# Differential attention: scores in three passes on split operands, value products one row later

## The chip, the cores and the metric

One core of a Trainium2 chip runs the whole program. The metric is the device time of one execution in microseconds (us). Three runs before the change took 2974.46, 2977.0 and 2977.47 us, median 2977.0.

## The reference

For a sequence of 1024 tokens of width 1024, three layers follow one another. The first has eight heads of forgetting attention (64 wide, causal, with a per-head decay added to the scores), a convolution and a pooling branch, then a feed-forward part. The second is retention. The third is differential attention. The two attentions matter here:

```python
# forgetting attention, for each block of 128 queries
s = einsum(q, k) * 64 ** -0.5 + cum[query] - cum[key]
p = softmax(where(key <= query, s, -1e30));  out = p @ v
# differential attention: 8 heads, each two halves of 64; q and k rotated (rope)
sc = einsum(q, k) * 64 ** -0.5          # for both halves
p = softmax(where(key_chunk <= query_chunk, sc, lowest))
out = (p[0] - lam * p[1]) @ v
```

Afterwards the output of a differential head is normalised over its 128 columns, scaled, and gated with a silu of a projection.

## The kernel before

Sizes: P = 128, S = 1024, NB = 8 blocks of 128 queries ("rows" t = 0 to 7), HALF = 512. The five engines run instruction streams of their own. The order on each is written out by hand, and they meet by counters: each finished step has a name (`s0_3`, `e1_2`, `pt0_4_1`), and the others wait for its number.

**Products to full precision.** The activations are split once into a high and a low part (HH, HL, type F32R), and each weight unit too (WH, WL; VectorE takes the difference at L255, `low_part`). `mm3` (L239 to L241) multiplies high by high, high by low and low by high into one sum. An F32 matmul on unsplit operands stands in the trace as two records, each with a weight load of its own.

**Attention.** `attend_pe`, `attend_act` and `attend_dve` serve both kinds. `forget` is true for the forgetting layer, where one iteration handles a pair of heads (three in a loop, the fourth in a last pass with `more` false). It is false for the differential layer, where one iteration is one head of two halves (seven in a loop, one last). For row t, TensorE does these steps:

- `projections(t)`: a part of the next head's q, k, v or gate, 24 matmuls of 512 columns for a whole half or 12 for part of one, into the bank DB. A plan by row says which.
- `turn(t)` (L764): the exponentials are transposed block by block into the banks TB, so that they can be stationary operands. With two forgetting heads this is done for head 0 and then head 1 through the same banks; the second waits until VectorE has copied the first into PT0 (L1056, `pt0_t_g`). A differential head has one set, the weights, which VectorE formed at L1035; it leaves the banks at L1051.
- `square_sums` (L794, forgetting only): sums of squares for the norm of the next q or k, into DB. ScalarE's copy and square precede them (L915, L917). Its logarithm (L923) and exponential (L925) follow, and DB is free for the next projection after the logarithm.
- `scores(t + 1)` (L810): both heads or halves, each on 64 of the 128 rows of the array, for the keys up to the row's end. Forgetting adds a bias (L818), and both add the mask (L822).
- `values(t)` (L852): the products of PT with the transposed v into the bank AO. They wait for `o{t-1}`, VectorE's output of the row before, which empties AO.

VectorE, for row t: copies out of the banks (`out_of_banks`), the gate (`gates`), the two row maxima of t + 1 (L1020), the scaled output (L1064 and L1066, or L1069), in the differential layer the weights of t + 1 (L1026 to L1035), the norm or rope of the next q or k, and in row 4 `low_part`. After row 7 come the copy of k into kT (L1099), `low_part`, and for a differential head its norm (L1981) and gating (L1987). ScalarE, for row t: the evacuation of a projection, then both exponentials of t + 1 (L960, in the order of the maxima), and at the head's end the silu, the copy of q into qT (L1010) and the squares of the output blocks (`block_out`, L1947).

Before the loops, `first_pe`, `first_act` and `first_dve` make the first head's q, k and v. q is copied at L1168 and k at L1190, and `warm` (L304) keeps TensorE busy. In the last forgetting pair `fill` puts the convolution's layer norm between the rows (`conv_pe`, L1222 and L1227; centring on VectorE at L1262, squares on ScalarE at L1236). In the last passes `warm` runs ahead of `turn`.

## Time and profile before

| | |
|---|---|
| median of 3 runs | 2977.0 us |
| profiled execution, in all | 2978.64 us |
| its span | 2976.6 us |
| TensorE busy | 2819.4 us (95%) |
| VectorE busy | 1609.3 us (54%) |
| ScalarE busy | 650.7 us (22%) |
| granted TensorE clock | 0.987 of full speed |

The span runs from the first to the last instruction of the profiled execution, and all later rows count from its start. Forgetting attention lies between about 172 and 496 us, differential attention between 2281 and 2856 us. A busy time is the union of an engine's instructions. What a change is worth depends on the engine that ends each wait, and so on the chain of waits.

### The profile page before, as it was taken

To read this page: it belongs to the slowest core of one execution; us is meant where nothing else is said; L and a number is where in the kernel's file an instruction comes from. 1 tells how busy PE (TensorE), PEld (TensorE's weight loads), DVE (VectorE), ACT (ScalarE), POOL (GpSimd) and SP (SyncE) were. 2 spreads that over 40 slices of the span, in tenths; PEclk is the share of its full clock that TensorE was granted. 3 is DMA by queue.
4 is the path that set the end of the run, shared out by engine and by line. 5 is a ranking of instruction groups with operands and counts; after the bars stand their busy time and mean duration, and the time that the engine had idled before them with its cause. 6 is when DMAs were issued, how large, how long until landed. Compare 5 with 4: busy or idle time off the path is not lost.

```text
span 2976.6 us, 35289 instructions
## 1 busy us (share of the span) xinstructions
PE 2819.4 (95%) x13352; PEld 2228.9 (75%) x13368; DVE 1609.3 (54%) x2062; ACT 650.7 (22%) x1152; POOL 299.1 (10%) x295
## 2 busy tenths in 40 slices
PE   8889999989999999999999999999998999999996
PEld 6656766768888888877888888888866777777664
DVE  7754445355554554564554454445374666666644
ACT  2133333121111111122111011011042333333321
POOL 0799700000000000001000000000000000000000
PEclk9999999999999999999999999999999999999998
DMA  4211111234443434333222222222242222222121
GB/s 165 88 38 57 56 43 71 99 113 143 140 155 127 165 139 146 141 113 142 85 70 85 85 70 70 92 77 79 77 170 89 71 70 70 71 72 71 50 113 71
DMA packets 48618, 286.61 MB, mean 96 GB/s; under 512 B 6576, under 2 KB 6704, under 8 KB 18608
## 3 DMA queue, kind: packets, MB, share of 16 engines
q1 hardware_dynamic: 21776, 118.50, 11.7%
q0 software_dynamic: 14544, 105.91, 10.4%
q10 hardware_dynamic: 12240, 61.39, 5.4%
q8 instruction: 40, 0.66, 0.1%
q14 instruction: 18, 0.15, 0.0%
HBM read 248.03 MB, written 29.36 MB: 93 GB/s over the span
## 4 chain that ended last, share of the span: by engine, by line
PE 81%; DVE 12%; issue 4%; ACT 2%; DMA 1%; DVEq 0%; SPq 0%; ACTq 0%
PE PB L239 12%; PE PB L241 12%; PE PB L240 12%; PE OBB L239 8%; PE OBB L241 8%; PE OBB L240 8%; PE OBB L852 3%; PE TBB L764 3%; PE PB L810 3%; PE TBB L239 2%; PE TBB L241 2%; PE TBB L240 2%; DVE small L1020 1%; DVE on L1830 1%; DVE cacc L1206 1%
## 5 line engine op out<-in xcount | busy, mean ns | idle before, releaser
L239 PE MATMUL PB<-HH,WH 128*128 128x512 f32 x1520 | 599.8, 395 | 25.6 <-issue 7.7
L241 PE MATMUL PB<-HH,WL 128*128 128x512 f32 x1520 | 594.8, 391 | 0.0
L240 PE MATMUL PB<-HL,WH 128*128 128x512 f32 x1520 | 594.8, 391 | 0.0
L239 PE MATMUL OBB<-HH,WH 128*128 128x512 f32 x992 | 399.6, 403 | 0.1
L241 PE MATMUL OBB<-HH,WL 128*128 128x512 f32 x992 | 387.3, 390 | 0.0
L240 PE MATMUL OBB<-HL,WH 128*128 128x512 f32 x992 | 386.7, 390 | 0.0
L239 PEld LDWEIGHTS PB<-HH,WH 128*128 128x128 f32 x1520 | 287.5, 189 | 93.1 <-issue 28.9
L240 PEld LDWEIGHTS PB<-HL,WH 128*128 128x128 f32 x1520 | 287.6, 189 | 61.9 <-issue 2.2
L241 PEld LDWEIGHTS PB<-HH,WL 128*128 128x128 f32 x1520 | 287.2, 189 | 60.5
L255 DVE TENSOR_TENSOR WL<-RAW,WH 128x2048 fp32r<-128x2048 f32 x101 | 233.1, 2308 | 61.9 <-DMA WH<-units 46.1
L2071 POOL DMA_DIRECT2D WH<-units x85 | 45.5, 535 | 1997.0 <-PE PB L239 1292.4
L241 PEld LDWEIGHTS OBB<-HH,WL 128*128 128x128 f32 x992 | 186.2, 188 | 40.2
L960 ACT ACTIVATE E<-PB,small 128x128 f32<-128x128 f32 (+3 forms) x192 | 140.8, 737 | 345.2 <-DVE small L1020 340.5
L239 PEld LDWEIGHTS OBB<-HH,WH 128*128 128x128 f32 x992 | 186.6, 188 | 35.9 <-DVE WL L255 0.3
L240 PEld LDWEIGHTS OBB<-HL,WH 128*128 128x128 f32 x992 | 186.7, 188 | 35.4
L1020 DVE TENSOR_REDUCE small<-PB 128x1 f32<-128x128 f32 (+3 forms) x192 | 136.2, 751 | 75.7 <-PE PB L822 75.7
L852 PE MATMUL OBB<-vt,PT 128*128 128x64 f32 (+1 forms) x1152 | 150.1, 281 | 11.2 <-DVE PT L1051 11.2
L852 PEld LDWEIGHTS OBB<-vt,PT 128*128 128x128 f32 x1152 | 137.7, 194 | 15.5 <-DVE PT L1051 15.5
L1551 DVE SCALAR_TENSOR_TENSOR G<-PB,par,G 128x1023 f32<-128x1023 f32 (+1 forms) x44 | 56.4, 1282 | 171.2 <-ACT G L1470 168.2
L2104 POOL TENSOR_TENSOR cacc<-cacc,prod 128x496 f32<-128x496 f32 (+29 forms) x90 | 131.2, 1459 | 0.0
L810 PE MATMUL PB<-kT,qT 64*128 64x512 f32 (+3 forms) x576 | 118.9, 517 | 4.9 <-DVE kT L1190 2.3
L764 PE MATMUL TBB<-con,E 128*128 128x128 f32 x576 | 88.5, 279 | 29.9 <-DVE PT L1056 19.6
(319 smaller groups left out, 3752.6 us busy)
## 6 DMA issues: line engine op xcount, KB each, us to landing
RAW<-units SPq DMA_DIRECT2D x85, 1024.0 KB, 4.8
WH<-units POOLq DMA_DIRECT2D x85, 1024.0 KB, 5.1
gs<-units ACTq DMA_DIRECT2D x16, 1024.0 KB, 4.8
gu<-gs ACTq DMA_DIRECT2D x16, 1024.0 KB, 3.9
RAW<-gu SPq DMA_DIRECT2D x16, 1024.0 KB, 4.8
WH<-gu POOLq DMA_DIRECT2D x16, 1024.0 KB, 5.4
tmpd<-xr SPq DMA_DIRECT2D x128, 64.0 KB, 2.0
A<-xT SPq DMA_DIRECT2D x4, 1024.0 KB, 9.8
```

The source lines that it names most:

```text
L239: first = pe.e.matmul(out, wh, xh, start=start, stop=False)
L240: pe.e.matmul(out, wh, xl, start=False, stop=False)
L241: return pe.e.matmul(out, wl, xh, start=False, stop=stop), first
L255: dve.e.tensor_tensor(WL[s][:, :], RAW[:, :], WH[s][:, :].bitcast(F32), ALU.subtract).then_inc(unit_split, 1)
L764: mm = pe.e.transpose(dst[:, c * P:(c + 1) * P], src(b), c_("ident"))
L810: pe.e.matmul(PB[c][:, b:b + w], qT[64 * c:64 * c + 64, t * P:(t + 1) * P], kT[64 * c:64 * c + 64, b:b + w], start=True, stop=False, skip_ ...
L852: mm = pe.e.matmul(AO[:, c * w:(c + 1) * w], (PT0, PT1)[c][:, b, :], vt[:, b, c * w:(c + 1) * w], start=b == 0, stop=b == t, skip_group_ch ...
L960: e.activation((E0, E1)[c][:, 0:n], PB[c][:, 0:n], ACT.Exp, bias=small[:, c, t:t + 1], accum_out=small[:, 2 + c, t:t + 1]).then_inc(act_do ...
L1020: e.tensor_reduce(small[:, c, t:t + 1], PB[c][:, 0:(t + 1) * P], AX, ALU.max, negate=True).then_inc(dve_done, dve.mark(f"m{c}_{t}"))
L1551: e.scalar_tensor_tensor(buf[:, j, d:], PB[b][:, 0:S - d], tap(tile, t, i), buf[:, j, d:], ALU.mult, ALU.add).then_inc(dve_done, dve.mark( ...
L2071: pool.dma_start(WH[n % 2][:, :], source.rearrange("u p n -> p (u n)")).then_inc(hi_full[n % 2], 16)
L2104: pool.tensor_tensor(cacc[:, c, a:b], cacc[:, c, a:b], prod[:, n % 2, 0:b - a], ALU.add).then_inc(conv_taps, 1)
```

## The change

In the differential layer the scores are computed as `mm3` does its products: q and k are split into high and low parts of type F32R (qh, ql, kh, kl), and each score block is the sum of three matmuls. A block of fewer than 256 columns is widened to 256. In the loop the parts are made in row 7 of the head before: high parts by ScalarE, low parts by VectorE. For the first head this is done in `first_act` and `first_dve`.

In both layers `values(t - 1)` follows `projections(t)`, and outputs move a row later on VectorE wherever `more` holds. In the forgetting layer the second head's transposes follow `scores(t + 1)`, and up to row 3 they have a bank of their own. The sums of squares come ahead of the scores from row 2 on and behind them in rows 0 and 1. VectorE copies the second head out between the two maxima. `block_out` follows the exponentials.

```diff
@@ -731,6 +731,10 @@
 kN = work("kN", [P, S], F32, 12 * K)
+qh = work("qh", [P, S], F32R, 0)
+kh = work("kh", [P, S], F32R, 4 * K)
+ql = at("ql", [P, S], F32R, 108 * K)
+kl = at("kl", [P, S], F32R, 28 * K)
 vF = work("vF", [P, S], F32, 16 * K)
@@ -804,7 +808,16 @@
                 pe.e.wait_ge(act_done, at_mark(pe, "act", f"e{c}_{t - 1}", i))
-        for b in range(0, n, HALF):
+        for b in range(0, n if not forget else 0, HALF):
+            w = max(256, min(HALF, n - b))
+            for q_part, k_part in ((qh, kh), (qh, kl), (ql, kh)):
+                for c in range(2):
+                    rows = slice(64 * c, 64 * c + 64)
+                    pe.e.matmul(PB[c][:, b:b + w], q_part[rows, t * P:(t + 1) * P],
+                                k_part[rows, b:b + w], start=q_part is qh and k_part is kh,
+                                stop=False, skip_group_check=True)
+        for b in range(0, n if forget else 0, HALF):
             w = min(HALF, n - b)
@@ -823,23 +836,30 @@
-    def turn(t):
-        if not more and t:
+    def turn_bank(t, c, g):
+        return TB[c if forget and t < 4 else g]
+    def turn(t, c):
+        if not more and t and not c:
             warm(pe, TB[0], 1 if forget else 2)
-        for c in range(2 if forget else 1):
-            src = (E0, E1)[c]
-            if forget:
-                pe.e.wait_ge(act_done, at_mark(pe, "act", f"e{c}_{t}", i))
-            for g in range(1 if t < 4 else 2):
-                if not forget:
-                    pe.e.wait_ge(dve_done, at_mark(pe, "dve", f"w{t}_{g}", i))
-                if c:
-                    pe.e.wait_ge(dve_done, at_mark(pe, "dve", f"pt0_{t}_{g}", i))
-                elif t:
-                    pe.e.wait_ge(dve_done, at_mark(pe, "dve", f"pt{int(forget)}_{t - 1}_{int(t > 4) * g}", i))
-                transposes(pe, TB[g], lambda b: src[:, b * P:(b + 1) * P],
-                           range(4 * g, min(4 * g + 4, t + 1)), f"T{c}_{t}_{g}")
+        src = (E0, E1)[c]
+        if forget:
+            pe.e.wait_ge(act_done, at_mark(pe, "act", f"e{c}_{t}", i))
+        for g in range(1 if t < 4 else 2):
+            if not forget:
+                pe.e.wait_ge(dve_done, at_mark(pe, "dve", f"w{t}_{g}", i))
+                if t:
+                    pe.e.wait_ge(dve_done, at_mark(pe, "dve", f"pt0_{t - 1}_{int(t > 4) * g}", i))
+            elif t < 4:
+                if t:
+                    pe.e.wait_ge(dve_done, at_mark(pe, "dve", f"pt{c}_{t - 1}_0", i))
+            elif c:
+                pe.e.wait_ge(dve_done, at_mark(pe, "dve", f"pt0_{t}_{g}", i))
+            else:
+                pe.e.wait_ge(dve_done, at_mark(pe, "dve", f"pt1_{t - 1}_{g}" if t > 4 else f"pt{g}_3_0", i))
+            transposes(pe, turn_bank(t, c, g), lambda b: src[:, b * P:(b + 1) * P],
+                       range(4 * g, min(4 * g + 4, t + 1)), f"T{c}_{t}_{g}")
@@ -873,9 +893,15 @@
+    def squares(t):
+        if forget and more:
+            for x, h in ended(plan, t, "qk"):
+                square_sums(pe, x, h, i)
+                last_evac[0] = f"r{x}{h}"
     if i is not None:
-        pe.e.wait_ge(act_done, at_last(pe, "act", "cq", i))
-        pe.e.wait_ge(dve_done, at_last(pe, "dve", "ck", i))
+        pe.e.wait_ge(act_done, at_last(pe, "act", "cq" if forget else "ck", i))
+        pe.e.wait_ge(dve_done, at_last(pe, "dve", "ck" if forget else "kl", i))
     scores(0)
@@ -888,18 +914,22 @@
         projections(t)
+        if t:
+            values(t - 1)
         if fill:
...
             pe.e.wait_ge(act_done, at_mark(pe, "act", "vt1", i))
-        turn(t)
-        if forget and more:
-            for x, h in ended(plan, t, "qk"):
-                square_sums(pe, x, h, i)
-                last_evac[0] = f"r{x}{h}"
+        turn(t, 0)
+        if t >= 2:
+            squares(t)
         if t + 1 < NB:
             scores(t + 1)
-        values(t)
+        if t < 2:
+            squares(t)
+        if forget:
+            turn(t, 1)
+    values(NB - 1)
     projections(NB)
@@ -961,6 +991,12 @@
+    def root_of(t):
+        if forget and more:
+            for x, h in ended(plan, t, "qk"):
+                norm_root_act(act, x, h, i)
+                busy[0] = f"N{x}{h}"
@@ -972,8 +1008,6 @@
                 norm_half_act(act, x, h, i)
-                norm_root_act(act, x, h, i)
-                busy[0] = f"N{x}{h}"
             else:
@@ -988,9 +1022,16 @@
                              ACT.Copy).then_inc(act_done, act.mark(f"vt{g}"))
-        elif block_out:
+        elif block_out and not more:
             block_out(t - 1)
+        if not forget and more and t == NB - 1:
+            e.wait_ge(dve_done, at_mark(act, "dve", "q1T", i))
+            e.activation(qh[:, :], qN[:, :], ACT.Copy, scale=0.125).then_inc(act_done, act.mark("cq"))
+            e.wait_ge(dve_done, at_mark(act, "dve", "k1T", i))
+            e.activation(kh[:, :], kN[:, :], ACT.Copy).then_inc(act_done, act.mark("ck"))
         halves_out(t)
+        if t >= 2:
+            root_of(t)
         if fill:
@@ -998,15 +1039,20 @@
         if t + 1 < NB:
-            for c in range(2):
-                exps(t + 1, c)
+            exps(t + 1, 0)
+        if t < 2:
+            root_of(t)
+        if t + 1 < NB:
+            exps(t + 1, 1)
+        if block_out and more and t:
+            block_out(t - 1)
     if not forget:
...
         e.preload_act_table_set(LN_EXP)
-    if more:
-        e.wait_ge(dve_done, at_mark(act, "dve", "Nq1" if forget else "q1T", i))
+    if more and forget:
+        e.wait_ge(dve_done, at_mark(act, "dve", "Nq1", i))
         e.activation(qT[:, :], qN[:, :], ACT.Copy, scale=0.125).then_inc(act_done, act.mark("cq"))
@@ -1042,20 +1088,19 @@
-    def out_of_banks(t):
-        for c in range(2 if forget else 1):
-            for g in range(1 if t < 4 else 2):
...
-                e.tensor_copy((PT0, PT1)[c][:, 4 * g:4 * g + k, :],
-                              TB[g][:, 0:k * P].rearrange("p (b n) -> p b n", n=P)).then_inc(
+    def out_of_banks(t, c):
+        for g in range(1 if t < 4 else 2):
...
+            e.tensor_copy((PT0, PT1)[c][:, 4 * g:4 * g + k, :],
+                          TB[c if t < 4 else g][:, 0:k * P].rearrange("p (b n) -> p b n", n=P)).then_inc(
@@ -1078,14 +1123,23 @@
     for t in range(NB):
-        out_of_banks(t)
+        out_of_banks(t, 0)
+        if not forget:
+            gates(t)
+        if t + 1 < NB:
+            maximum(t + 1, 0)
+        if forget:
+            out_of_banks(t, 1)
         if fill:
             fill(t)
-        gates(t)
         if t + 1 < NB:
-            maximum(t + 1, 0)
             maximum(t + 1, 1)
-        outputs(t)
+        if not more:
+            outputs(t)
+        elif t:
+            outputs(t - 1)
+        if not forget and more and t == NB - 1:
+            low_scores(dve, i)
         if t < len(early) and early[t] is not None:
@@ -1094,10 +1148,21 @@
-        e.wait_ge(dve_done, at_mark(dve, "dve", "Nk1" if forget else "k1T", i))
-        e.tensor_copy(kT[:, :], kN[:, :]).then_inc(dve_done, dve.mark("ck"))
+        outputs(NB - 1)
+        if forget:
+            e.wait_ge(dve_done, at_mark(dve, "dve", "Nk1", i))
+            e.tensor_copy(kT[:, :], kN[:, :]).then_inc(dve_done, dve.mark("ck"))
         low_part(dve, u0 + 4, i, 2)
+def low_scores(dve, i):
+    dve.e.wait_ge(act_done, at_mark(dve, "act", "cq", i))
+    dve.e.scalar_tensor_tensor(ql[:, :], qN[:, :], 0.125, qh[:, :].bitcast(F32),
+                               ALU.mult, ALU.subtract).then_inc(dve_done, dve.mark("ql"))
+    dve.e.wait_ge(act_done, at_mark(dve, "act", "ck", i))
+    dve.e.tensor_tensor(kl[:, :], kN[:, :], kh[:, :].bitcast(F32),
+                        ALU.subtract).then_inc(dve_done, dve.mark("kl"))
@@ -1165,8 +1230,11 @@
     act.e.wait_ge(dve_done, at_mark(act, "dve", "Nq1" if forget else "q1T"))
-    act.e.activation(qT[:, :], qN[:, :], ACT.Copy, scale=0.125).then_inc(act_done, act.mark("cq"))
+    act.e.activation((qT if forget else qh)[:, :], qN[:, :], ACT.Copy, scale=0.125).then_inc(
+        act_done, act.mark("cq"))
     if not forget:
+        act.e.wait_ge(dve_done, at_mark(act, "dve", "k1T"))
+        act.e.activation(kh[:, :], kN[:, :], ACT.Copy).then_inc(act_done, act.mark("ck"))
         act.e.wait_ge(pe_done, at_mark(act, "pe", "rtok"))
@@ -1186,8 +1254,12 @@
                 taps(dve, range(*{("q", 0): (12, 14), ("q", 1): (14, 15), ("k", 0): (15, 16)}[x, h]))
-    dve.e.wait_ge(dve_done, at_mark(dve, "dve", "Nk1" if forget else "k1T"))
-    dve.e.tensor_copy(kT[:, :], kN[:, :]).then_inc(dve_done, dve.mark("ck"))
+    if forget:
+        dve.e.wait_ge(dve_done, at_mark(dve, "dve", "Nk1"))
+        dve.e.tensor_copy(kT[:, :], kN[:, :]).then_inc(dve_done, dve.mark("ck"))
+    else:
+        dve.e.wait_ge(spilled, 16 + 64)
+        low_scores(dve, None)
     low_part(dve, u0 + 2)
```

## Rows read from the trace of the kernel before

**Rows 1.** Windows: busy us (instructions) of PE, PEld, DVE, ACT, POOL; clock, DMA, GB/s
```profile
172.00:400.00 228.00, 209.15 (x1212) 156.31 (x1222) 111.90 (x193) 70.69 (x156) 166.49 (x144) 1.00 0.14 49
...
2354.00:2792.00 438.00, 423.68 (x2280) 324.29 (x2278) 275.09 (x506) 147.26 (x372) 6.33 (x12) 1.00 0.23 72
```
**Rows 2.** Waits of the run: in total, times, longest
```profile
PE TBB L764 <- DVE PT L1056: 19.6, 32, 1.0
```
**Rows 3.** Timeline, forgetting rows 4 and 7: start, us, instruction, count, idle before
```profile
301.38 0.71 PE L764 MATMUL TBB<-con,E 128*128 128x128 f32 x5
302.77 0.77 PE L764 MATMUL TBB<-con,E 128*128 128x128 f32 x5 [0.68 <-DVE PT L1056]
303.46 1.56 PE L810 MATMUL PB<-kT,qT 64*128 64x512 f32 x8
...
333.51 1.03 PE L764 MATMUL TBB<-con,E 128*128 128x128 f32 x8
334.89 1.25 PE L764 MATMUL TBB<-con,E 128*128 128x128 f32 x8 [0.35 <-DVE PT L1056]
```
**Rows 4.** Chain of waits in one differential head: start, us, what
```profile
2539.99 0.97 DVE small L1020
...
2564.36 2.05 PE OBB L852 x16
```
**Rows 5.** Timeline, scores of a differential row 7: weight loads (PEld), matmuls
```profile
2554.99 0.30 PEld L810 LDWEIGHTS PB<-kT,qT 64*128 64x128 f32 x4 [0.17 <-issue]
2555.52 0.19 PEld L810 LDWEIGHTS PB<-kT,qT 64*128 64x128 f32 x2 [0.24 <-issue]
...
2554.99 1.99 PE L810 MATMUL PB<-kT,qT 64*128 64x512 f32 x8
```
**Rows 6.** Timeline, two of the matmuls of a dense product
```profile
2259.50 0.39 PE L239 MATMUL TBB<-HH,WH 128*128 128x512 f32 x1
2259.73 0.39 PE L240 MATMUL TBB<-HL,WH 128*128 128x512 f32 x1
```
**Rows 7.** Groups by line and form: count, busy us, mean ns, idle before
```profile
L396 DVE SCALAR_TENSOR_TENSOR tmn<-A,par,rbn 128x1024 f32<-128x1024 f32 x16 | 20.4, 1284 | 4.9 <-ACT rbn L345 4.5
...
L389 DVE TENSOR_TENSOR HL<-tmn,HH 128x1024 fp32r<-128x1024 f32 x16 | 19.5, 1220 | 0.0
...
L381 ACT ACTIVATE HH<-tmn 128x1024 fp32r<-128x1024 f32 x16 | 17.0, 1060 | 21.9 <-DVE tmn L396 21.6
```
**Rows 8.** Timeline, the end of a differential head
```profile
2566.45 0.35 DVE L1069 TENSOR_SCALAR ot<-OBB,small 128x128 f32<-128x128 f32 x1 [2.15 <-PE OBB L852]
...
2569.52 1.22 DVE L1981 TENSOR_TENSOR ot<-ot,small 128x1024 f32<-128x1024 f32 x1
...
2571.71 1.04 PE L764 MATMUL TBB<-con,ot 128*128 128x128 f32 x8
```
**Rows 9.** Timeline, ahead of the first differential head
```profile
2280.44 0.69 DVE L1190 COPY kT<-kN 128x1024 f32<-128x1024 f32 x1
...
2281.61 0.49 PE L810 MATMUL PB<-kT,qT 64*128 64x128 f32 x4 [0.26 <-issue]
```
**Rows 10.** Timeline, transposes of row 7 in the last differential head
```profile
2846.96 1.32 PE L764 MATMUL TBB<-con,E 128*128 128x128 f32 x8 [1.56 <-DVE E L1035]
```
**Rows 11.** Timeline, sums of squares and logarithm in a forgetting row 0
```profile
269.18 1.12 PE L794 MATMUL OBB<-sqh,con 128*128 128x512 f32 x2 [0.35 <-ACT sqh L917]
...
270.35 0.69 ACT L923 ACTIVATE rbh<-OBB,epsc 128x512 f32<-128x512 f32 x1 [1.22 <-PE OBB L794]
```
**Rows 12.** Timeline, forgetting row 7: evacuation, values, output
```profile
335.59 1.29 DVE L1056 COPY PT<-TBB 128x512 f32<-128x512 f32 x2 [0.15 <-PE TBB L764]
335.99 3.68 PE L852 MATMUL OBB<-vt,PT 128*128 128x64 f32 x32
...
340.00 0.28 DVE L1066 TENSOR_SCALAR ot<-OBB,small 128x64 f32<-128x64 f32 x1
```
**Rows 13.** Timeline, last forgetting pair: the convolution's variance sum
```profile
438.94 3.53 PE L1227 MATMUL OBB<-csq,ones 128*128 128x512 f32 x4 [0.73 <-ACT csq L1236]
```

More of the change, by code:

```diff
@@ L1043, in gates @@
                         dve_done, dve.mark(f"rawg{h}"))
-            def out_of_banks(t):
-                for c in range(2 if forget else 1):
-                    for g in range(1 if t < 4 else 2):
-                        k = min(4, t + 1 - 4 * g)
-                        e.wait_ge(pe_done, at_mark(dve, "pe", f"T{c}_{t}_{g}", i))
-                        if not forget:
-                            e.tensor_tensor(PT0[:, 4 * g:4 * g + k, :],
-                                            TB[g][:, 0:k * P].rearrange("p (b n) -> p b n", n=P),
-                                            rtok[:, 4 * g:4 * g + k].unsqueeze(2).to_broadcast([P, k, P]),
-                                            ALU.mult).then_inc(dve_done, dve.mark(f"pt{c}_{t}_{g}"))
-                            continue
-                        e.tensor_copy((PT0, PT1)[c][:, 4 * g:4 * g + k, :],
-                                      TB[g][:, 0:k * P].rearrange("p (b n) -> p b n", n=P)).then_inc(
-                                          dve_done, dve.mark(f"pt{c}_{t}_{g}"))
+            def out_of_banks(t, c):
+                for g in range(1 if t < 4 else 2):
+                    k = min(4, t + 1 - 4 * g)
+                    e.wait_ge(pe_done, at_mark(dve, "pe", f"T{c}_{t}_{g}", i))
+                    if not forget:
+                        e.tensor_tensor(PT0[:, 4 * g:4 * g + k, :],
+                                        TB[g][:, 0:k * P].rearrange("p (b n) -> p b n", n=P),
+                                        rtok[:, 4 * g:4 * g + k].unsqueeze(2).to_broadcast([P, k, P]),
+                                        ALU.mult).then_inc(dve_done, dve.mark(f"pt{c}_{t}_{g}"))
+                        continue
+                    e.tensor_copy((PT0, PT1)[c][:, 4 * g:4 * g + k, :],
+                                  TB[c if t < 4 else g][:, 0:k * P].rearrange("p (b n) -> p b n", n=P)).then_inc(
+                                      dve_done, dve.mark(f"pt{c}_{t}_{g}"))
             def outputs(t):
@@ L1080, in attend_dve @@
             for t in range(NB):
-                out_of_banks(t)
+                out_of_banks(t, 0)
+                if not forget:
+                    gates(t)
[3 more added lines that the diff above has]
+                    out_of_banks(t, 1)
                 if fill:
                     fill(t)
-                gates(t)
                 if t + 1 < NB:
-                    maximum(t + 1, 0)
                     maximum(t + 1, 1)
-                outputs(t)
+                if not more:
[4 more added lines that the diff above has]
+                    low_scores(dve, i)
                 if t < len(early) and early[t] is not None:
```

## Prediction

> **What bounds the kernel now.** The busy times by stage come first: the change touches attention only, which is two stages, and in both TensorE is busy over nine tenths of the time at a granted clock of 1.00 [rows 1]. So time can be won only where TensorE waits in attention, or where it computes slower than it needs to. The waits, summed over the run, name the first kind: TensorE sat 19.6 us in 32 waits before transposes until VectorE had copied the previous ones out of the bank [rows 2]. These are the forgetting heads (four pairs, eight rows each, one wait a row). Two rows in full [rows 3]: in row 4 the first head's five transposes start at 301.38 and the second's at 302.77; five take 0.55 us (0.109 each: eight and their 0.16 us tail fill the row of 1.03), so 0.84 us is lost though the idle time says 0.68, since a record's tail covers the rest. In row 7 it is 0.51. Measured so, a loop pair loses 0.55, 0.68, 0.81, 0.94, 0.84, 0.72, 1.05 and 0.51 us in its rows, and the last pair 6.26 us in rows 0 to 6.
>
> For differential attention the chain of waits is the view [rows 4]. Up to the scores of row 5 a head is TensorE alone. From 2539.99, where VectorE takes the maximum of row 5, to 2564.36, where the last products with the values start, the chain runs through VectorE and the exponentials, with TensorE off it. Then it is TensorE again. What TensorE saves between these two points is waited off again; what it saves before or after counts.
>
> **Step 1, scores in three passes.** Before, both half-heads' full-precision matmuls run side by side on 64 rows each: row 7 issues 8 records, four pairs, for 1024 columns, 1.99 us with their tail [rows 5]. At 2.4 GHz that is 4 x 1024 / 2400 = 1.71 us, 0.43 a pair and 0.213 per block of 128 columns. The split operands run one pass per column: in a dense product a 512-column matmul starts 0.23 us after the one before [rows 6]. No row shows split operands on half the array. I take pairs side by side at that rate, 0.228 us per 512 columns and 0.12 per 256, so three passes take 0.68 in place of 0.85 and, for 256 columns, 0.36 in place of 0.21 (row 0, and the tails of row 4, where the change widens 128 to 256) or of 0.43. Rows 0 to 7 then change by -0.15, +0.06, +0.13, +0.17, +0.03, +0.24, +0.27, +0.34 us (plus is won). In a loop head only rows 0 to 5 count: 0.48. The bounds are from the same rows: 0.213 per pair, a little more won (0.25 a head), and no overlap between halves at all, six passes at 0.228.
>
> Here a rule bears on it. In rows 5 four loads, so the second pair's two among them, are done by 2555.29, and the third pair's start at 2555.52, as the second pair of matmuls takes over from the first. So a load runs under a matmul of its own half, and I add nothing for loads. The Trainium skill ("TensorE: Matmul & The Clock Gate", Measured speedup vs the span model) says that a load overlaps running matmuls only when the row group differs. By that rule each pass would carry its load in the open; it is a rival below. The trace doesn't agree with it.
>
> **Step 2, operands.** ScalarE gets a copy (kh, 1.06 us), VectorE ql 1.28 and kl 1.22 [rows 7] for a key copy of 0.68. In loop heads they stand in row 7 on VectorE, behind the last transposes' evacuation, where it sat 2.15 us until the products were done [rows 8]. After them come outputs, split and normalisation as before, and TensorE has a projection of 24 matmuls meanwhile (5.5 us at rows 6's 0.23): normalisation ended 2570.74, TensorE took its result at 2571.71 [rows 8]. By my count it ends some 0.6 later: covered, with 0.4 us left. If that is used up, 0.6 a head at most. Before head 0 there is no cover. k is ready at 2280.44 and scores start at 2281.61 [rows 9]; now copy 1.06 and difference 1.22 follow each other, so scores start at about 2282.95: 1.35 us lost, once. DMAs are neither added nor moved.
>
> **Step 3, values after the next projection, differential heads.** TensorE's waits for PT in rows 5 and 6 go, but in the stretch that VectorE bounds: nothing. Values still wait for the output of the row before, because it empties their bank, and that output is now one row later on VectorE. For row 7 it comes after the last evacuation: one scaling of 0.35 us [rows 8], less its start-up, 0.28 us lost on the path. A loop head wins 0.48 - 0.28 = 0.20; seven, 1.4 us. In the last head TensorE waits for the weights in every later row, up to 1.56 us [rows 10], so each score's gain shortens the chain: 0.06 + 0.13 + 0.17 + 0.03 + 0.24 + 0.27 + 0.34, less 0.15 for row 0: 1.1 us. Its row 1 is held up by values 0 behind a projection, but two 0.85 us warm-up matmuls stand there as cover.
>
> **Step 4, forgetting heads, rows 0 and 1.** The evacuation waits go (0.55 + 0.68), so does the 0.57 us wait for the squares in row 0 (idle 0.35 by the row, the tail on top [rows 11]), and 0.22 between transposes and sums in row 1: 2.02. The sum of squares now follows the next scores; it takes 1.06 us, ScalarE starts its logarithm 1.17 after its start and needs 0.69 [rows 11]. Only then may the next projection use the bank, and between them lies one short transpose where before lay scores and values. Row 0: sums at 269.18, done 270.24, transpose until 270.35, projection at 271.08: 0.73 lost, besides 0.26 for the squares. Row 1: in addition ScalarE does an exponential first, 0.93. Together 1.92 in place of 2.02: +0.10.
>
> **Step 5, rows 2 to 6.** Second transposes come after the scores, whose main matmuls alone take 1.56 us in row 4 [rows 3], longer than the evacuation (at most 1.29 [rows 12], 0.97 there): 0.81 + 0.94 + 0.84 + 0.72 + 1.05 = 4.36 won. But VectorE's queue is now maximum, second evacuation, second maximum, output of the row before, and the output frees the bank for values. Row 6 waits about 0.47 for it, row 7 about 0.67, since their half projections (12 matmuls, 2.8 us) are shorter than that queue.
>
> **Step 6, row 7.** It has no scores: its 0.51 stays. And values 7 wait for outputs 6, which VectorE now does after both evacuations. These end at 336.88 (335.59 + 1.29), two outputs take 0.48; values started at 335.99 and will at 337.50 [rows 12]. That is 1.50 lost. A loop pair wins 0.10 + 4.36 - 0.47 - 0.67 - 1.50 = 1.82; three, 5.5 us.
>
> **Step 7, last forgetting pair.** Its evacuation waits in rows 1 to 6 go: 5.6. It has no projection, so values wait for the second evacuation: about 2.0 over the rows. The convolution's centring and squares on VectorE now come behind maximum and second evacuation. The variance sum, at 438.94 after 0.73 us of idle [rows 13], comes about 0.96 later in spite of the wait won in row 0, its twin in row 3 about 1.85 later. Won: 0.8 us.
>
> **Sum.** 5.5 + 0.8 + 1.4 + 1.1 - 1.35 = 7.45 us. The profiled execution has a span of 2976.6 and took 2978.64 in all; less 7.45 it is 2971.2. The median of the runs is 2977.0, 1.64 below it, so **2969.6 us**. Some 0.2%, about 6 us, is what a measurement of this kernel can tell from no change.
>
> **Rivals.** (a) New waits eat the forgetting heads' gain. For: outputs and root stand in queues where nothing is left over. Against: 4.36 us a pair is read off row by row. Worth 6.3 us: 2976. Chance 0.22. (b) The outputs' queue costs less (values 6 and 7 not delayed by rows 5 and 6), and pairs run at 0.213: three times 1.1, eight times 0.25, 1 in the last pair, some 6 us more: 2963. Chance 0.12. (c) On the other side: passes don't pair well on half the array. With each pair's load in the open (0.11: four loads take 0.30 us in rows 5, one 0.19) a 512-column pass takes 0.32, a 256-column one 0.21; rows 0 to 5 lose 1.76 us a head in place of winning 0.48, so 7 x 2.24 and 3.3 in the last: 2988.5. That is what the skill's rule would give. With halves one after the other it is six passes, 3.9 us a head worse and 6 in the last: 3003. For: no such row exists. Against: rows 5, where halves share the array. The price decides from a 512-column pair of about 0.28 us on. Chance 0.14 (0.08 and 0.06). That VectorE bounds most of a differential head is in the sum already.
>
> **Numbers.** The forecast has 0.52 (its own range 2965 to 2974). The range for all takes in (a), (b) to 2961 and the first half of (c): 2961 to 2990. Under 2971.0 lies most of the forecast's half and (b), over 2983.0 only (c): faster 0.52, same 0.34, slower 0.14.
>
> **What would show it.** Pairs of score passes 0.21 to 0.24 us apart in row 7; the waits for L1056 gone in seven of eight rows; a TensorE gap before L239 after the sums of squares in rows 0 and 1; values 7 of a forgetting pair starting 0.6 us after the last PT copy; first differential scores 2.5 us after k. If a differential loop head is shorter than 72.7 us, or a forgetting one longer than the old, steps 3 or 4 to 6 are wrong; if score passes are 0.3 us apart or more, step 1 is.

## The result and the profile after

The changed kernel took 2987.9 us in the median of 9 runs, the kernel before 2978.2 beside it: a ratio of 1.0027, 95% interval 1.0017 to 1.0036. It is **slower by some 9 us**, where 7.45 us less was forecast (2969.6). One of the nine runs took 6609.3 us, a slow one that the ratio leaves out; without it the median is 2987.2. The range (up to 2990) holds it; the sign had a chance of 0.14, and that for another mechanism. The profiled execution took 2990.11 us with a span of 2988.3, 11.7 more than before.

Lines have moved: transposes L764 are L768, values L852 are L872, evacuations L1056/L1051 are L1101/L1096, outputs L1066/L1069 are L1111/L1114, and the three passes are L817. First the windows of attention, which answer to [rows 1], then four short ones (busy us of PE, PEld, DVE, ACT and POOL with instructions, granted clock, DMA share, GB/s):

```profile
172.00:400.00 228.00, 217.08 (x1227) 163.09 (x1227) 104.60 (x189) 73.40 (x158) 168.34 (x145) 0.96 0.14 49
246.00:260.00 14.00, 12.83 (x54) 11.25 (x55) 6.69 (x9) 0.00 (x0) 13.61 (x11) 0.63 0.00 0
335.70:340.50 4.80, 4.74 (x32) 4.75 (x33) 0.00 (x1) 0.00 (x0) 4.64 (x5) 0.75 0.00 0
340.50:344.50 4.00, 4.00 (x11) 3.14 (x11) 3.61 (x4) 0.00 (x0) 3.92 (x4) 0.50 0.00 0
420.00:431.00 11.00, 9.83 (x48) 8.71 (x47) 4.76 (x8) 0.00 (x0) 0.00 (x0) 0.69 0.00 0
...
2360.00:2798.00 438.00, 417.26 (x2416) 335.62 (x2415) 281.98 (x510) 150.72 (x375) 6.33 (x12) 1.00 0.22 72
```

TensorE is busier in the forgetting heads than before, 217.08 us against 209.15. Busy time also grows where waits go, since more work then fits into the window; but here there are nearly as few matmul records as before (1227 for 1212), so each took longer. The column of the clock says why: 0.96 where it had been 1.00. The fall is not spread out: by the clock's record in the trace it begins at 249.3, 338.1 and 423.4, once a loop pair and 0.9 to 2.3 us after values 7 have begun, and lasts 10.24, 6.83 and 6.83 us, at half speed (1.2 GHz). Next TensorE's waits, summed over the run:

```profile
PE OBB L872 <- DVE ot L1114: 11.6, 18, 1.1
...
PE OBB L872 <- DVE ot L1111: 4.5, 6, 1.2
...
PE OBB L239 <- ACT rbh L953: 4.2, 6, 0.7
...
PE TBB L768 <- DVE PT L1101: 3.0, 4, 2.0
PE OBB L239 <- DVE sg L1088: 2.9, 15, 0.2
...
PE PB L817 <- DVE kl L1164: 2.6, 1, 2.6
```

The 19.6 us in 32 waits of [rows 2] are down to 3.0 in 4, so the change does what it says. In their place stand waits for outputs (L1111 forgetting, L1114 differential), for the root (L953), and one that the prediction doesn't have at all: projections (L239) that wait for the gates (L1088).

The timeline of a forgetting row 7, TensorE and then VectorE, answers to [rows 3] and [rows 12]:

```profile
335.76 5.01 PE L872 MATMUL OBB<-vt,PT 128*128 128x64 f32 x32 [1.17 <-DVE ot L1111]
340.52 0.77 PE L239 MATMUL OBB<-HH,WH 128*128 128x512 f32 x1
...
341.95 0.63 PE L239 MATMUL OBB<-HH,WH 128*128 128x512 f32 x1
...
343.23 0.63 PE L239 MATMUL OBB<-HH,WH 128*128 128x512 f32 x1
...
334.03 1.29 DVE L1101 COPY PT<-TBB 128x512 f32<-128x512 f32 x2 [0.15 <-PE TBB L768]
335.24 0.27 DVE L1109 TENSOR_SCALAR ot<-OBB,small 128x64 f32<-128x64 f32 x1
335.43 0.27 DVE L1111 TENSOR_SCALAR ot<-OBB,small 128x64 f32<-128x64 f32 x1
```

Values 7 wait for the two output scalings behind the last evacuation, as step 6 has it. What follows was not foreseen: they take 5.01 us instead of 3.68, and of the projection's matmuls every third starts 1.28 us after the last, so one in 0.427, where [rows 6] has 0.23. Before, 0.35 us of idle time stood ahead of the second transposes and none ahead of the values; now 0.35 and 1.17 stand within 2.8 us, and the clock falls behind them.

The split scores of a differential row 7, loads and then matmuls, answer to [rows 5]:

```profile
2492.65 0.19 PEld L817 LDWEIGHTS PB<-kl,qh 64*128 64x128 f32 x2
2492.88 0.19 PEld L817 LDWEIGHTS PB<-kh,ql 64*128 64x128 f32 x2
2493.12 0.19 PEld L817 LDWEIGHTS PB<-kh,qh 64*128 64x128 f32 x2
...
2492.54 0.50 PE L817 MATMUL PB<-kh,qh 64*128 64x512 f32 x2
2492.88 0.40 PE L817 MATMUL PB<-kl,qh 64*128 64x512 f32 x2
2493.11 0.39 PE L817 MATMUL PB<-kh,ql 64*128 64x512 f32 x2
2493.34 0.40 PE L817 MATMUL PB<-kh,qh 64*128 64x512 f32 x2
```

From the second on, pairs start 0.23 us apart, and each pair's loads run while the pair before, on the same rows, is still under way. This row did not exist before; it settles rival (c).

Last, the end of a differential loop head, a projection behind row 1's scores, and the pause ahead of the first head ([rows 9]):

```profile
2446.10 0.50 PE L239 MATMUL OBB<-HH,WH 128*128 128x512 f32 x1 [0.21 <-DVE sg L1088]
...
2497.65 1.82 PE L872 MATMUL OBB<-vt,PT 128*128 128x128 f32 x14 [0.45 <-DVE ot L1114]
...
2502.24 1.94 PE L872 MATMUL OBB<-vt,PT 128*128 128x128 f32 x15 [1.12 <-DVE ot L1114]
...
2289.38 0.39 PE L817 MATMUL PB<-kh,qh 64*128 64x256 f32 x2 [2.60 <-DVE kl L1164]
```

**Where the time went.** ScalarE's evacuation of the transposed values marks each pair and head: two of them, a head apart, in the changed kernel:

```profile
2439.31 0.60 ACT L1023 ACTIVATE vt<-TBB 128x512 f32<-128x512 f32 x1
...
2512.71 0.60 ACT L1023 ACTIVATE vt<-TBB 128x512 f32<-128x512 f32 x1
```

From these marks: three forgetting loop pairs 259.25 us (256.93 before), so +2.3 where -5.5 was forecast; the last pair, from the transposes of its values to those of its outputs, 64.22 (62.85), +1.4 for -0.8; key ready to first scores 2.8 (1.2), +1.6 for +1.35; the seven differential loop heads 515.48 (510.44), +5.0 for -1.4; the last head to the end of the span 180.79 (181.91), -1.1 as forecast. These make +9.2. The rest of the span's 11.7 lies where nothing was changed, mostly in half-clock stretches near the start and in the feed-forward part, which move from one execution to the next.

### The profile page after: what moved, and what is told of

The parts are those of the page before. It is cut to its first block, busy times and chain, and to the rows that moved or that the text cites. A ratio compares the mean times of both kernels' runs of the same rounds, so it can differ in the third digit from the quotient of the medians.

```text
span 2988.3 us, 35698 instructions
## 1 busy us (share of the span) xinstructions
PE 2827.7 (95%) x13560; PEld 2258.8 (76%) x13560; DVE 1614.4 (54%) x2070; ACT 659.6 (22%) x1160; POOL 299.6 (10%) x295
## 4 chain that ended last, share of the span: by engine, by line
PE 79%; DVE 13%; issue 4%; ACT 3%; DMA 1%; DVEq 0%; SPq 0%; ACTq 0%
PE PB L239 12%; PE PB L240 12%; PE PB L241 11%; PE OBB L239 8%; PE OBB L241 8%; PE OBB L240 8%; PE OBB L872 3%; PE TBB L768 3%; PE TBB L239 2%; PE TBB L241 2%; PE TBB L240 2%; DVE small L1066 2%; PE PB L823 1%; PE PB L817 1%; DVE on L1902 1%
## 5 line engine op out<-in xcount | busy, mean ns | idle before, releaser
L239 PE MATMUL PB<-HH,WH 128*128 128x512 f32 x1520 | 601.1, 395 | 25.5 <-issue 7.7
L239 PE MATMUL OBB<-HH,WH 128*128 128x512 f32 x992 | 403.6, 407 | 8.2 <-ACT rbh L953 4.2
L239 PEld LDWEIGHTS PB<-HH,WH 128*128 128x128 f32 x1520 | 288.1, 190 | 93.6 <-issue 28.7
L239 PEld LDWEIGHTS OBB<-HH,WH 128*128 128x128 f32 x992 | 188.5, 190 | 49.5 <-ACT rbh L953 6.6
L1066 DVE TENSOR_REDUCE small<-PB 128x1 f32<-128x128 f32 (+3 forms) x192 | 138.4, 750 | 74.1 <-PE PB L835 74.1
L872 PEld LDWEIGHTS OBB<-vt,PT 128*128 128x128 f32 x1152 | 146.7, 199 | 34.9 <-DVE ot L1114 19.6
L872 PE MATMUL OBB<-vt,PT 128*128 128x64 f32 (+1 forms) x1152 | 153.9, 285 | 18.9 <-DVE ot L1114 11.6
L1623 DVE SCALAR_TENSOR_TENSOR V<-PB,par,V 128x1023 f32<-128x1023 f32 (+1 forms) x44 | 56.4, 1282 | 105.6 <-ACT V L1546 102.6
L1096 DVE TENSOR_TENSOR PT<-TBB,rtok 128x512 f32<-128x512 f32 (+2 forms) x96 | 50.5, 553 | 113.4 <-PE TBB L768 113.3
```

What stands on the lines that cost most here:

```text
L239: first = pe.e.matmul(out, wh, xh, start=start, stop=False)
L872: mm = pe.e.matmul(AO[:, c * w:(c + 1) * w], (PT0, PT1)[c][:, b, :], vt[:, b, c * w:(c + 1) * w], start=b == 0, stop=b == t, skip_group_ch ...
L1066: e.tensor_reduce(small[:, c, t:t + 1], PB[c][:, 0:(t + 1) * P], AX, ALU.max, negate=True).then_inc(dve_done, dve.mark(f"m{c}_{t}"))
L1096: e.tensor_tensor(PT0[:, 4 * g:4 * g + k, :], TB[g][:, 0:k * P].rearrange("p (b n) -> p b n", n=P), rtok[:, 4 * g:4 * g + k].unsqueeze(2). ...
L1623: e.scalar_tensor_tensor(buf[:, j, d:], PB[b][:, 0:S - d], tap(tile, t, i), buf[:, j, d:], ALU.mult, ALU.add).then_inc(dve_done, dve.mark( ...
```

## Experiments

All times are medians against 2977.5 to 2978.1 us for the kernel before beside them. Theory: the forgetting heads lose to the clock that falls behind the wait of values 7; the differential heads lose to the values' new place, not to the passes.

**e1: outputs 6 first.** VectorE, row 7:

```diff
+                if more and t == NB - 1:
+                    outputs(t - 1)
                 out_of_banks(t, 0)
...
-                elif t:
+                elif t and not (more and t == NB - 1):
                     outputs(t - 1)
```

> The changed kernel, but in row 7 of every loop pair and loop head VectorE does outputs 6 ahead of the evacuation of row 7's transposes. Theory A (a wait, and the clock that falls after it): values 7 no longer wait about 1.2 us for outputs 6; the granted clock then stays 1.00 after values 7 of the three forgetting loop pairs, where the changed kernel's trace shows stretches of 10.24, 6.83 and 6.83 us at half of it. Half of 23.9 us is 11.9, the waits are 3.5: 15.5 us less, 2972.5. Theory B (the half clock comes from something else in the reordered rows): only the waits go, 3.5 us and 0.3 x 7 in the differential heads, 2982, and the half-clock stretches stay. Theory C (outputs first only moves the wait to the transposes' copies): no change, 2988.

Measured: 2970.0 us, ratio 0.9971 (0.9961 to 0.9981), 18 less than the changed kernel and faster than the kernel before. Its windows and row 7:

```profile
172.00:400.00 228.00, 220.94 (x1295) 164.67 (x1294) 108.37 (x199) 76.32 (x163) 167.51 (x146) 1.00 0.16 56
...
328.08 1.25 PE L768 MATMUL TBB<-con,E 128*128 128x128 f32 x8 [0.38 <-DVE PT L1101]
329.17 3.68 PE L872 MATMUL OBB<-vt,PT 128*128 128x64 f32 x32
```

The clock is 1.00 again, values 7 take 3.68 and start without a wait. The three pairs take 243.85 us, 13.1 less than before. Two instructions of 0.27 us each, in another place of one queue, carry most of the difference between slower and faster. Theory A, a little more than expected.

**e2: the wait stays, the idle time doesn't.**

```diff
+            if forget and more:
+                warm(pe, PB[0], 1)
             values(NB - 1)
```

> The changed kernel with one warm-up matmul (a bank that is not read) ahead of values 7 in forgetting loop pairs: VectorE's queue and the wait for outputs 6 stay, but TensorE is not idle before it. Theory A: the wait stays, the half-clock stretches are gone or shorter: 12 us less, 2976. Theory B: the stretches stay, 2988 or a little more.

Measured: 2976.0 us, ratio 0.9997 (0.9984 to 1.001).

```profile
172.00:400.00 228.00, 219.50 (x1278) 163.10 (x1276) 109.70 (x198) 76.45 (x164) 169.32 (x146) 1.00 0.16 55
...
331.47 1.02 PE L304 MATMUL PB<-con 128*128 128x512 f32 x2
332.80 3.79 PE L872 MATMUL OBB<-vt,PT 128*128 128x64 f32 x32 [0.31 <-DVE ot L1113]
```

Work that nobody reads, put ahead of the values in three places, wins 12 us: it does nothing but fill the pause. So the price of the wait has two parts, now measured apart: the pairs take 259.25, 247.96 (e2) and 243.85 us (e1), 11.3 for the clock and 4.1 for the wait itself. It didn't go so in every run: two of the twelve took 2986.9 and 2989.3 us at a mean clock of 0.983 and 0.982, as long as the changed kernel, and no trace shows where they lost it.

**e3: the three passes alone**, on the kernel before: qh, kh, ql, kl and the three-pass loop as in the diff, values and outputs where they were; in VectorE's row 7:

```diff
+                if not forget and more and t == NB - 1:
+                    low_scores(dve, i)
                 outputs(t)
```

> The kernel before with the three-pass scores and their operands, and none of the reordering. Theory A (the passes pay off, and the loop head's loss of 0.47 us comes from the values behind the projection): a loop head is 0.48 us shorter than before (72.45), the first differential head pays 1.35 for the operands and some 1.7 for a clock that falls in the longer pause, the last wins about 1: 2978.2 + 3.0 - 3.4 - 1.1 = 2976.7. Rival (passes or operands cost the loop heads): a loop head stays at 73.4 or so, 2978.2 + 3.0 + 3.3 = 2984.5.

Measured: 2976.2 us, ratio 0.9996 (0.9988 to 1.0005). A loop head takes 72.47 us by the same marks:

```profile
2427.63 0.60 ACT L1002 ACTIVATE vt<-TBB 128x512 f32<-128x512 f32 x1
...
2500.08 0.59 ACT L1002 ACTIVATE vt<-TBB 128x512 f32<-128x512 f32 x1
```

That is 0.46 less than 72.93 (0.48 by step 1), with ql and kl standing in VectorE's row 7: the passes win what was forecast, and step 2's cover holds in the old order. The changed kernel's 73.40 is 0.93 worse, so the values' place costs that. Before the first head TensorE was idle 0.94 us here, and the clock stayed up.

**e4: the forgetting order alone**, differential attention as before. Its core:

```diff
-                if t:
+                if t and forget:
                     values(t - 1)
...
+                else:
+                    values(t)
```

> The changed kernel's order in the forgetting pairs; differential attention as in the kernel before (full-precision scores, values right after the scores). Theory A: the reordered pairs give back their 4.4 us each by the root wait, the wait before values 7 and the half clock behind it; half-clock stretches after values 7 stay, the differential loop period is 72.93 again: 2978.2 + 3 = 2981. Rival (the half clock needs something of the differential part's other placement, or the pairs win as forecast): 2978.2 - 6.3 = 2972.

Measured: 2983.9 us, ratio 1.0015 (1.0006 to 1.0024). The half-clock stretches are there, 6.83 us behind values 7 of each loop pair, and a differential head takes 72.95. The forgetting order alone makes the kernel slower, 3 us more than I had put; the rival is out.

**e5: squares ahead of the scores in rows 0 and 1 too**, on e1:

```diff
-                if t >= 2:
-                    squares(t)
+                squares(t)
                 if t + 1 < NB:
                     scores(t + 1)
-                if t < 2:
-                    squares(t)
```

> e1_out6_first, with the sums of squares ahead of the next scores (and the roots ahead of both exponentials) in rows 0 and 1 of the forgetting loop pairs too, as in the other rows. Theory A (step 4 of the prediction): the projections' waits for the root, idle 0.67 and 0.74 by the changed kernel's trace and 1.7 with tails, go, and 0.57 + 0.22 come back as waits of the sums for the squares: 0.9 to 1.1 us less a pair, 3 us less than e1's 2970.0, so 2967. Rival (the exponential behind the roots holds up the next transposes and scores by as much as is won): 2970 or more, with the idle time moved from the projection's first matmul to the transposes or scores.

Measured: 2968.0 us, ratio 0.9965 (0.9952 to 0.9979), not to be told from e1 by these intervals. In the traces a pair is 0.04 to 0.15 us shorter. The same row 0, first in the changed kernel, then in e5:

```profile
272.17 1.12 PE L798 MATMUL OBB<-sqh,con 128*128 128x512 f32 x2
...
274.07 0.50 PE L239 MATMUL OBB<-HH,WH 128*128 128x512 f32 x1 [0.67 <-ACT rbh L953]
```

```profile
267.59 1.12 PE L798 MATMUL OBB<-sqh,con 128*128 128x512 f32 x2 [1.07 <-ACT sqh L944]
...
269.66 0.47 PE L239 MATMUL OBB<-HH,WH 128*128 128x512 f32 x1
```

The sums wait 1.07 for their squares where the projection waited 0.67 for its root. The wait changes its place, not its size (1.07 and 0.56 in the two rows, for 0.67 and 0.74 idle). The median lies nearer to theory A's 2967 than to the rival's 2970, but not by theory A: the first differential head, where the clock stayed up (see e8), is 1.6 us shorter than in e1. By the pairs theory A is wrong: it took the wait for the squares at the old 0.57 [rows 11], though nothing lies ahead of the sums now but one transpose. For the pairs the rival's outcome came, by a wait that neither named. And an idle 1.07 us behind a whole projection did not bring the clock down.

**e6: values 0 and 1 early again**, differential loop heads, on e1:

```diff
-                if t:
+                if t and (forget or not more or t > 2):
                     values(t - 1)
...
                 if forget:
                     turn(t, 1)
+                elif more and t < 2:
+                    values(t)
```

> e1_out6_first, with values 0 and 1 of a differential loop head back behind the scores of rows 1 and 2, so that they stand between scores and projection again. Theory A (what the loop heads lose is the projection's wait for VectorE's evacuation of the gates from its bank): the waits of 0.21 and 0.18 us ahead of projections 1 and 2 go or shrink to what the kernel before had, and the loop head is shorter than e1's 73.09 by what values hide, 0.3 to 0.7 us: 2965 to 2968. Rival (the loss is in rows 5 to 7, where VectorE bounds the head): the waits move to other rows and the head stays at 73.0 to 73.1, 2970.

Measured: 2973.9 us, ratio 0.9985 (0.9976 to 0.9994); the loop head is longer, 74.1. The projections no longer wait for the gates, but:

```profile
2432.81 0.71 PE L872 MATMUL OBB<-vt,PT 128*128 128x128 f32 x4 [1.45 <-DVE ot L1116]
```

Values 1 now wait for outputs 0, which I had left one row late on VectorE. Neither theory had that: the experiment moved one half of a pair that has to move together. It is mended in e10.

**e7: the values' place without the passes**, on e1: scores and operands of differential attention as before.

```diff
-                for b in range(0, n if not forget else 0, HALF):
+                for b in range(0, 0, HALF):
...
-                for b in range(0, n if forget else 0, HALF):
+                for b in range(0, n, HALF):
```

> e1_out6_first with full-precision scores and their old operands in differential attention: of the change there, only the values' place is left. Theory A (passes win 0.46 us a head and the place loses what is between 73.09 and 72.47, whatever the passes do): loop head 73.09 + 0.46 = 73.55, but no second operand copy before head 0, 1.35 to 3 us less there: 2970.0 + 3.2 + 1.1 - 2.5 = 2971.8. Rival (the place loses only because the operands' differences stand in VectorE's row 7, so that nothing is lost without them): loop head 72.9, 2967.

Measured: 2970.1 us, ratio 0.9971 (0.996 to 0.9982). Loop head 73.53 (theory A: 73.55; rival: 72.9). With outputs 6 first the place costs 0.6 us a head over 72.93, with or without the passes.

**e8: two more warm-up matmuls ahead of the first differential head**, on e1:

```diff
-                warm(pe, TBB, 5)
+                warm(pe, TBB, 7)
```

> e1_out6_first with two more warm-up matmuls ahead of the first differential scores, where TensorE was idle for 2.6 us and the granted clock then fell to half for 3.41 us. Theory A: the clock stays at 1.00 through the first head, 1.7 us less: 2968.3, and the first head takes 72.2 (vt to vt) instead of 73.5. Rival (the clock there doesn't hang on that pause): 3.41 us at half remain, 2970.

Measured: 2968.1 us, ratio 0.9968 (0.9955 to 0.998); first head 71.90, clock 1.00. The number is theory A's, but e5's trace has 71.89 with the old warm-up, so this run alone doesn't show it. All traces together do better. Idle time before that head is not the same in each, since in some the warm-up runs at half clock and ends later:

```profile
2273.25 0.39 PE L817 MATMUL PB<-kh,qh 64*128 64x256 f32 x2 [1.97 <-DVE kl L1159]
```

That is e5. The clock fell behind idle times of 2.60 (the changed kernel), 2.6 (e1) and 2.5 us (e9), and not behind 2.0 (e5, e6), 1.0 (e2), 0.9 (e3) and 0.4 (e8).

**e9: the convolution's work behind the second maximum**, last forgetting pair, on e1:

```diff
-                if fill:
-                    fill(t)
                 if t + 1 < NB:
                     maximum(t + 1, 1)
+                if fill:
+                    fill(t)
```

> e1_out6_first, with the work that VectorE does for the convolution in the last forgetting pair behind the second maximum instead of between the second evacuation and that maximum. Theory A (step 7 missed that 2.35 us of it now stand ahead of the second maximum, whose exponential, weights and evacuation everything in the next row waits for): the 1.95 us wait for PT in row 7 shrinks to about 0.4, those for E in rows 4 to 6 of 0.4 to 0.5 shrink, the variance sums come later than now by up to 1.2 each; the last pair (62.5 us from scores 0's end to its last transposes, 61.3 in the kernel before less its half-clock stretch) is 1 to 3 us shorter, 2967 to 2969. Rival (VectorE has simply too much to do there, the order doesn't matter): 62.5 stays, 2970.

Measured: 2965.6 us, ratio 0.996 (0.9948 to 0.9972). VectorE and then TensorE, rows 6 and 7 of the last pair, in the changed kernel (e1 has the same order and waits) and in e9:

```profile
488.93 1.15 DVE L1101 COPY PT<-TBB 128x512 f32<-128x512 f32 x2
489.99 2.35 DVE L1345 TENSOR_TENSOR cl<-cacc,ch 128x1024 fp32r<-128x1024 f32 x2
492.26 1.22 DVE L1066 TENSOR_REDUCE small<-PB 128x1 f32<-128x1024 f32 x1
...
495.65 1.16 PE L768 MATMUL TBB<-con,E 128*128 128x128 f32 x8 [1.96 <-DVE PT L1101]
```

```profile
470.39 1.21 DVE L1066 TENSOR_REDUCE small<-PB 128x1 f32<-128x1024 f32 x1
471.52 2.35 DVE L1347 TENSOR_TENSOR cl<-cacc,ch 128x1024 fp32r<-128x1024 f32 x2
...
475.06 1.16 PE L768 MATMUL TBB<-con,E 128*128 128x128 f32 x8 [0.97 <-DVE PT L1101]
```

The wait halves, those for E are gone, and the pair takes 60.58 us for e1's 62.52. It shrank to 0.97, not to 0.4: outputs 6 now stand behind the convolution and hold up VectorE's evacuation of row 7's transposes. Theory A with that correction; 1.9 us are shown by the trace, the rest of the median's 4.3 less than e1 is within what the intervals leave open.

**e10: e6 with outputs 0 and 1 early as well**, and with e5's and e8's edits:

```diff
-                if not more:
+                if not more or (not forget and t < 2):
                     outputs(t)
-                elif t and not (more and t == NB - 1):
+                elif t and (forget or t > 2) and not (more and t == NB - 1):
                     outputs(t - 1)
```

> e6_values_early_rows_0_1 with VectorE's outputs 0 and 1 back in their own rows too, since there values 1 waited 1.45 us for outputs 0; with e5's order of squares and e8's longer warm-up. Theory A (the gate wait of rows 1 and 2 is what the new place costs, 0.73 us a head, and e6 only put outputs' wait in its stead): loop head 73.09 - 0.73 = 72.4, seven of them 5 us less, and e8 and e5 give 1 to 2 more than e1: 2963 to 2964. Rival (another wait takes its place again): loop head 73.0 or more, 2968.

Measured: 2966.4 us, ratio 0.9962 (0.995 to 0.9974), 2 to 3 us above what I put. The loop head is what it should be:

```profile
2418.69 0.60 ACT L1022 ACTIVATE vt<-TBB 128x512 f32<-128x512 f32 x1
...
2491.15 0.60 ACT L1022 ACTIVATE vt<-TBB 128x512 f32<-128x512 f32 x1
```

72.46 here, 72.41 to 72.46 in five. The gate wait is worth 0.64 us a head.

**e11: the old differential order throughout**, with e1's, e5's and e8's edits:

```diff
-                if t:
+                if t and forget:
                     values(t - 1)
```

> The forgetting pairs of e1 with outputs 6 first, three-pass scores, and in differential attention the order of the kernel before for values and outputs; e5's order of squares and e8's longer warm-up. Theory A (parts are additive): loop head 72.47 as in e3, last head as e3, 2970.0 - 7 x 0.62 - 1 to 2 = 2964. Rival (the moved values pay off in the last head or elsewhere outside the loop, so that both placements end equal): 2967.

Measured: 2966.4 us, ratio 0.9955 (0.9942 to 0.9968). The number is the rival's 2967 rather than theory A's 2964, but the loop head is theory A's, 72.44 to 72.48, the same as e10's: with the gate wait removed, the new place in rows 2 to 7 neither wins nor loses. What the traces differ in is the clock: e11's has half-clock stretches of 10.24 us at 480.6 and of 6.83 us at 2839.2 that e10's doesn't have.

**e12: e10 and e9 together** (both edits as above).

> e10_early_values_and_outputs with e9's place for the convolution's work on VectorE. If the parts are additive: e10's traces show a loop head of 72.43 and forgetting pairs of 80.1, 81.0 and 82.4, and e9's a last pair of 60.6 in place of 62.5: 2966.4 less 2 to 4 is 2962 to 2964, some 15 us faster than the kernel before. Rival (what e9's median won over e1's beyond the 1.9 us in its trace came with the phase of the clock near the start and the feed-forward part, not from the edit): 2964.5.

Measured: 2966.3 us, ratio 0.9958 (0.9942 to 0.9973). No gain over e9 or e10 alone can be told. Its trace shows the parts where they should be (72.48 a head; 80.1, 81.1 and 82.4 a pair), but the last pair takes 63.89 us for e9's 60.58, with half-clock stretches of 3.41 us at 427.5 and 444.6 that e9's doesn't have. So neither view is settled by the median: the edit's gain stands in the rows, and the clock took it back in this trace.

The first of these stretches, at 426 to 429, stands in the traces of e5, e10, e11 and e12, all with e5's order, and in none of e1, e6, e7, e8 and e9. Yet e5's order changes rows 0 and 1 of the loop pairs only. In the 60 us ahead of this place e1's and e5's matmuls start at the same distances from one another, to 0.05 us, and the waits are the same too; first e1, then e5:

```profile
428.56 1.99 PE L1301 MATMUL OBB<-csq,ones 128*128 128x512 f32 x4 [1.42 <-ACT csq L1310]
```

```profile
429.13 3.62 PE L1294 MATMUL OBB<-csq,ones 128*128 128x512 f32 x4 [1.42 <-ACT csq L1303]
```

The same four matmuls behind the same wait take 1.99 us at full clock and 3.62 at half. The length of the waits alone doesn't decide whether the clock falls; what else does is not shown here. What is shown is that this group of kernels, e5 and e8 to e12, lies at 2965.6 to 2968.1 us, 10 to 12 below the kernel before and 20 to 22 below the change as made.

## Why the prediction was wrong

By its own steps:

- **Step 1** was right: 0.46 us a loop head by e3 for 0.48, 1.1 in the last head for 1.1 (e1 against e7, which differ there only in the passes and their operands: 179.41 and 180.57 us from its mark to the end of the span). Pairs at 512 columns lie 0.23 us apart. The Trainium skill ("TensorE: Matmul & The Clock Gate", The mechanism, the section just ahead of the one that the prediction names) says a load overlaps running matmuls only on another row group; the load rows of L817 don't agree with it, as those of [rows 5] had not. The median landed at rival (c)'s 2988.5, but not by rival (c): a right number would have been no proof of it.
- **Step 2**: the loop heads' cover held; the first head paid 1.6 us for 1.35, and in the traces of the changed kernel, e1 and e9 some 1.6 to 1.7 more, because the pause had grown to 2.5 us or more and the clock fell behind it.
- **Step 3 failed.** It counted the waits for PT, E and outputs, and not what the values had been hiding. In the old order they stood between row t+1's scores and the next projection, just while VectorE emptied the gates' bank, which that projection needs. Moved behind it, they uncovered a wait of 0.21 and 0.18 us by the rows, 0.64 with tails (e1 against e10). The 0.28 us for outputs 7's queue was right: e1 took it away and a head fell from 73.40 to 73.09. Seven heads: +5.0 instead of -1.4, of which some 1.7 is the clock in the first. I asked what the values wait for and never what waits behind them.
- **Step 4** was right in effect. From the first projection's start to the third's, a loop pair took 19.46 to 19.54 us before and 18.43 to 18.46 in e1, to which values 1 (8 matmuls of 0.109 us) have to be added: 0.14 to 0.21 won for 0.10. The other order of sums and scores (e5) is equal within 0.15 us.
- **Step 5** was undersized: without waits for outputs 6 and without the clock, a pair wins 4.4 us (e1), where steps 4 to 6 without their 1.50 give 3.32. By the starts of the projections, with the values' matmuls at 0.109 us as above, rows 2 to 6 won 4.95 us for 3.89: rows 2 to 5 some 0.14 to 0.19 more each than put, and row 6 another 0.39, since values 5 don't wait for outputs at all there, where 0.47 was put.
- **Step 6 failed, and decided the sign.** The wait is there with the place forecast, and its own price of 4.1 us in three pairs (4.5 forecast) was right. What was left out is the clock: 11.3 us in three pairs (e2). I priced the wait in idle microseconds and carried the clock of 1.00 over from [rows 1], the very column that the wait changed.
- **Step 7 failed**: +1.4 for -0.8. I had the convolution's work come later, and priced only the two sums behind it, not the 2.35 us that then stand ahead of the second maximum (e9).

Forecast and result differ by 17.1 us by the medians. The pairs' clock makes 11.3 of it, from which step 5's surplus (3.1) and the slightly smaller wait (0.4) come off; the differential loop heads make 6.4, the last pair 2.2, the first head's operands 0.3: 16.7. Of what was listed to look for, the waits of L1056 gone, the 0.23 us and the gap ahead of L239 came, and so did a forgetting pair longer than the old (86.42 us for 85.64 in the mean of three), which pointed at steps 4 to 6. The list had no sign for what step 3 missed: it names a differential head shorter than 72.7 us, not a longer one, and it became 73.40.

## What to carry to other kernels

Price a new wait of TensorE twice: once in idle time, and once for what the granted clock does behind it. Here another short wait lay just ahead each time; whether it takes both was not tried. A couple of matmuls whose result nobody reads, or one short instruction put earlier in the other engine's queue, can be worth more than the wait itself (here 15.4 us for three waits of 1.17). When work is moved away from a place, ask what it was covering there, and move both ends of a hand-over (here the products and the scaling that frees their bank) together.

## What the hardware showed

- Behind an idle 0.35 and 1.17 us, with 1.25 us of short transposes between them and 64-column matmuls after them, TensorE's granted clock fell from 2.4 to 1.2 GHz for 6.83 to 10.24 us, in all three loop pairs of the changed kernel's trace and of e4's; with the pause filled (e2) or the second wait gone (e1) it didn't. Behind a single idle 1.07 us between a projection and more dense work (e5) it didn't either.
- Idle time alone doesn't decide it: behind the same 0.37 and 1.42 us, around the same instructions, the clock fell for 3.41 us in e5's trace and not in e1's.
- At half clock 512-column matmuls of a dense product start 0.427 us apart, at full clock 0.23, so a stretch costs a little under half of its length (6.83 us: about 3.1).
- The two 64-row halves of split operands share the array as full-precision ones do: 0.23 us a pair at 512 columns.
